# The last down projection third by third of the tokens, with the final norm of five token tiles between its blocks

## What is computed

```python
h2 = _rmsnorm(x, norm2_w) * (1 + scale2) + shift2
f = (jax.nn.silu(h2 @ w_ffn_gate) * (h2 @ w_ffn_up)) @ w_ffn_down
x = x + gate2 * f
...
def _rmsnorm(x, w):
    y = x * lax.rsqrt(jnp.mean(x * x, axis=-1, keepdims=True) + EPS)
    return y * w
```

## Time and profile before

| what | value |
|---|---|
| median of three runs | 2498.18 us (2493.07 to 2500.6) |
| span of the profiled execution | 2492.5 us |
| TensorE busy | 2334.4 us (94%) |
| VectorE busy | 1269.8 us (51%) |
| ScalarE busy | 623.7 us (25%) |
| GpSimd busy | 104.9 us (4%) |
| transfers | 258.75 MB, mean 104 GB/s |

### The profile page before, as it was taken

The page is one execution under the profiler, slowest core; times in us unless marked ns, Lnnn a source line. Parts: engine busy times, 40 slices in busy tenths (PEclk is TensorE's granted clock), DMA queues, the critical chain, the costliest instruction groups (busy, mean ns, idle before and its releaser), DMA issues.

```text
span 2492.5 us, 36698 instructions
## 1 busy us (share of the span) xinstructions
PE 2334.4 (94%) x13811; PEld 2252.1 (90%) x13811; DVE 1269.8 (51%) x2056; ACT 623.7 (25%) x1007; POOL 104.9 (4%) x151
## 2 busy tenths in 40 slices
PE   5699999998899999998999897989999999999995
PEld 5599999998799999988999896879999999999995
DVE  6665544555566767635557545543334434333345
ACT  1423223432333232322121423221111111111111
POOL 0000000000111111101000000010000000000000
PEclk9699999999899999988999998999999999999997
DMA  6265523332555465642223333211111111111104
GB/s 192 71 192 161 169 65 89 89 97 83 176 180 178 157 191 179 199 133 86 87 87 120 108 132 127 85 55 48 42 42 42 42 50 42 42 42 44 48 25 152
DMA packets 319867, 258.75 MB, mean 104 GB/s; under 512 B 13443, under 2 KB 293701, under 8 KB 319807
## 3 DMA queue, kind: packets, MB, share of 16 engines
q1 hardware_dynamic: 263535, 204.11, 27.1%
q10 hardware_dynamic: 52368, 41.57, 5.3%
q0 software_dynamic: 3904, 12.26, 1.4%
HBM read 195.69 MB, written 62.21 MB: 103 GB/s over the span
## 4 chain that ended last, share of the span: by engine, by line
PE 50%; issue 43%; DVE 4%; ACT 1%; DMA 1%; POOL 1%; SPq 0%; ACTq 0%; DVEq 0%; POOLq 0%
PE PS L988 28%; PE PS L1144 11%; PE PS L1126 2%; PE PS L1194 2%; PE PS L1120 1%; PE PS L1123 1%; DVE ada_sum L1382 1%; DVE hf L1400 1%; PE PS L1110 1%; PE PS L1133 1%; PE PS L1029 1%; PE PS L1067 1%; DMA ada_first<-in_w_ada 0%; PE PS L1205 0%; DVE pool_s L1653 0%
## 5 line engine op out<-in xcount | busy, mean ns | idle before, releaser
L988 PE MATMUL PS<-act_a_hi,w_hi 128*128 128x364 f32 (+1 forms) x1344 | 448.4, 334 | 25.2 <-DVE act_a_lo L1613 15.1
L1340 DVE TENSOR_TENSOR w_lo<-w_raw,w_hi 128x1024 fp32r<-128x1024 f32 x156 | 195.5, 1253 | 493.8 <-ACT w_hi L641 492.1
L988 PE MATMUL PS<-act_a_lo,w_hi 128*128 128x364 f32 (+1 forms) x1344 | 445.4, 331 | 0.0
L988 PE MATMUL PS<-act_a_hi,w_lo 128*128 128x364 f32 (+1 forms) x1344 | 445.2, 331 | 0.0
L1286 PE MATMUL PS<-act_b_lo,w_hi 128*128 128x364 f32 (+1 forms) x1056 | 347.7, 329 | 0.0
L1286 PE MATMUL PS<-act_b_hi,w_hi 128*128 128x364 f32 (+1 forms) x1056 | 347.5, 329 | 0.0
L1286 PE MATMUL PS<-act_b_hi,w_lo 128*128 128x364 f32 (+1 forms) x1056 | 347.5, 329 | 0.0
L641 ACT ACTIVATE w_hi<-w_raw 128x1024 fp32r<-128x1024 f32 x156 | 164.7, 1056 | 488.0 <-PE PS L988 213.0
L988 PEld LDWEIGHTS PS<-act_a_hi,w_hi 128*128 128x128 f32 x1344 | 256.2, 191 | 27.8 <-DVE act_a_lo L1613 16.4
L988 PEld LDWEIGHTS PS<-act_a_lo,w_hi 128*128 128x128 f32 x1344 | 256.1, 191 | 0.0
L988 PEld LDWEIGHTS PS<-act_a_hi,w_lo 128*128 128x128 f32 x1344 | 255.9, 190 | 0.0
(11 more groups left out here) (249 smaller groups left out, 3442.2 us busy)
## 6 DMA issues: line engine op xcount, KB each, us to landing
w_raw<-in_w_in SPq DMA_DIRECT2D x64, 512.0 KB, 5.2
acs_in<-acs_c SPq DMA_DIRECT2D x36, 512.0 KB, 5.4
ada<-in_w_ada SPq DMA_DIRECT2D x16, 1024.0 KB, 7.4
gp_s<-gp ACTq DMA_DIRECT2D x24, 544.0 KB, 3.4
w_raw<-in_w_ffn_gate SPq DMA_DIRECT2D x22, 512.0 KB, 3.8
w_raw<-in_w_ffn_up SPq DMA_DIRECT2D x22, 512.0 KB, 3.8
w_raw<-in_w_ffn_down SPq DMA_DIRECT2D x22, 512.0 KB, 3.6
xs_in<-xs_c SPq DMA_DIRECT2D x36, 256.0 KB, 3.0
```

The costliest lines, as they stand in the source:

```text
L988: e = pe.matmul(PS[:, n, 0:w], wt[a], at_[b][:, o:o + w], start=(k == 0 and q == 0), stop=(k == len(steps) - 1 and q == 2))
L1340: dve.tensor_tensor(w_split[v][1][:, :], w_raw[v][:, :], w_split[v][0][:, :].bitcast(F32), ALU.subtract)\
```

## The change

The 24 blocks of the last pair are put in another order: for each third, all eight channel tiles (block i has third i // 8, down unit i // 4 % 2, and PSUM bank i % 3). After 8 blocks the first 364 tokens have their whole sum, which covers token tiles 0 and 1; after 16 blocks 728 tokens, which covers tiles 2, 3 and 4. Their turns stand in TensorE's list behind blocks 9, 11, 17, 19 and 21, and their adds and variances in VectorE's list behind sums 10 to 22. The turns of tiles 5 to 8 stand behind the last block.

SP loads all nine x2 tiles into nine buffers fx of their own as soon as the last up unit is through, then the gain; all nine loads count on one semaphore. The add works in place in fx. For the five early tiles ScalarE multiplies by the power in place, and GpSimd multiplies by the gain in place. For the other four VectorE multiplies by both, as before, but in place. The small per-tile values have a column for each tile (small3). SP stores the tiles in their order.

```diff
+    small3 = keep("small3", [P, 3, NCH])
...
-    (fx0, fx1, fr0, fr1, fjunk, fo0, fo1, final_w) = region(
+    *fx, fjunk, final_w = region(
+        RB, RC, *[(f"fx{t}", [P, KT, P], F32) for t in range(NCH)], ("fjunk", [P, KT, P], F32),
+        ("final_w", [P, KT, P], F32))
...
+    EARLY = 5
+    LAST = [8, 8, 16, 16, 16, 24, 24, 24, 24]
...
-            sp.wait_ge(mm["ffn"], FFN_SUBS)
+            sp.wait_ge(mm["ffn"], FFN_SUBS - 24)
+            for t in range(NCH):
+                L = CH if t < NCH - 1 else DEC
+                sp.dma_start(fx[t][0:L, :, :], x2_s[t][0:L, :].rearrange("t (f c) -> t f c", c=P)).then_inc(f_landed, 16)
             sp.dma_start(final_w[:, :, :], A["final_norm_w"].rearrange("(f c) -> f c", c=P).partition_broadcast(P))\
               .then_inc(fw_in, 16)
...
+            for t in range(NCH):
+                if t < EARLY:
+                    sp.wait_ge(f_pool, t + 1)
+                else:
+                    sp.wait_ge(f_dve, t - EARLY + 1)
...
+            final_power(0)
+            pool.wait_ge(fw_in, 16)
+            for t in range(EARLY):
+                final_power(t + 1)
+                pool.wait_ge(f_scaled, t + 1)
+                pool.tensor_tensor(fx[t][:, :, :], fx[t][:, :, :], final_w[:, :, :], ALU.mult).then_inc(f_pool, 1)
+            for t in range(EARLY + 1, NCH):
+                final_power(t)
...
+            final_squares(0)
+            for t in range(EARLY):
+                final_squares(t + 1)
+                act.wait_ge(f_rms, t + 1)
+                act.activation(fx[t][:, :, :], fx[t][:, :, :], ACT.Copy, scale=small3[:, 2, t:t + 1]).then_inc(f_scaled, 1)
+            for t in range(EARLY + 1, NCH):
+                final_squares(t)
...
-            for v in range(2):
-                down(U_END - 2, FFN_DVE - 24, v)
...
+            def last_down(i):
+                n, v, m = i // 8, i // 4 % 2, i % 4
+                o, w = SUBS[n]
+                unit_ready(U_END - 2 + v)
+                pe.wait_ge(mm_free["ffn"], FFN_DVE - 24 + i + 1)
+                for k in range(2):
+                    for q, (a, b) in enumerate(PASSES):
+                        e = pe.matmul(PS[:, i % 3, 0:w], w_split[v][a][:, k * 512 + m * P:k * 512 + (m + 1) * P],
+                                      f_split[b][:, k, o:o + w], start=(k == 0 and q == 0), stop=(k == 1 and q == 2))
+                e.then_inc(mm["ffn"], 1)
+
+            def final_turn(t):
                 L = CH if t < NCH - 1 else DEC
+                pe.wait_ge(mm_free["ffn"], FFN_DVE - 24 + 3 + LAST[t])
                 if t >= 2:
-                    pe.wait_ge(n3.added, t - 1)
+                    pe.wait_ge(f_added, t - 1)
...
+            turn_after = {9: 0, 11: 1, 17: 2, 19: 3, 21: 4}
+            for i in range(24):
+                last_down(i)
+                if i in turn_after:
+                    final_turn(turn_after[i])
+            for t in range(EARLY, NCH):
+                final_turn(t)
...
+            def final_add(t):
+                L = CH if t < NCH - 1 else DEC
+                if t == 0:
+                    dve.wait_ge(f_landed, 16 * NCH)
+                dve.wait_ge(f_turned, t + 1)
...
+            add_after = {10: 0, 12: 1, 18: 2, 20: 3, 22: 4}
+            var_after = {12: 0, 14: 1, 20: 2, 22: 3}
+            for i in range(24):
+                last_sum(i)
+                if i in var_after:
+                    final_var(var_after[i])
+                if i in add_after:
+                    final_add(add_after[i])
             dve.wait_ge(fw_in, 16)
...
+            for t in range(EARLY, NCH):
+                final_add(t)
+                final_var(t - 1)
+                if t > EARLY:
+                    final_scale(t - 1)
+            final_var(NCH - 1)
+            final_scale(NCH - 1)
```

More of the change, by code:

```diff
@@ L470, in _ @@
                 load_unit(U_END - 2 + v, v, wd[:, 2 * FG - 2:2 * FG, v * 512:(v + 1) * 512])
-            sp.wait_ge(mm["ffn"], FFN_SUBS)
+            sp.wait_ge(mm["ffn"], FFN_SUBS - 24)
+            for t in range(NCH):
+                L = CH if t < NCH - 1 else DEC
+                sp.dma_start(fx[t][0:L, :, :], x2_s[t][0:L, :].rearrange("t (f c) -> t f c", c=P)).then_inc(f_landed, 16)
             sp.dma_start(final_w[:, :, :], A["final_norm_w"].rearrange("(f c) -> f c", c=P).partition_broadcast(P))\
               .then_inc(fw_in, 16)
[L476 to L485, removed]
-            for v in range(2):
[L488 to L499, removed]
+            for t in range(NCH):
[4 more added lines that the diff above has]
+                L = CH if t < NCH - 1 else DEC
+                dst = yo_p[t * CH:(t + 1) * CH, :] if t < NCH - 1 else yo_s
+                sp.dma_start(dst.rearrange("t (f c) -> t f c", c=P), fx[t][0:L, :, :]).then_inc(out_sem, 16)
+            sp.wait_ge(out_sem, 16 * NCH)
         @block.gpsimd
@@ L619, in norm2_tiles @@
                     powers(n2, t, v, L)
-            def norm3_tiles(tiles, L):
-                for t, v, i in tiles:
-                    powers(n3, t, v, L)
             pairs(norm2_tiles)
@@ L965, in _, with final_squares @@
             hi(U_END - 1, 1, "ffn", FFN_SUBS - 24)
[L968 to L976, removed]
+            def final_squares(t):
+                L = CH if t < NCH - 1 else DEC
+                act.wait_ge(f_added, t + 1)
+                act.wait_ge(f_squared, t)
+                act.activation(fjunk[0:L], fx[t][0:L], ACT.Square, accum_out=small3[0:L, 0, t:t + 1]).then_inc(f_squared, 1)
+            final_squares(0)
[5 more added lines that the diff above has]
+                final_squares(t)
         @block.tensor
@@ L1847, in _ @@
             dve.wait_ge(mm_free["ffn"], FFN_DVE - 24)
[L1848 to L1861, removed]
-                                         final_w[0:L, :, :], ALU.mult, ALU.mult).then_inc(n3.scaled, 1)
@@ L1878, in _, with last_sum @@
-            norm3_scale(8, 0, 64, DEC)
+            def last_sum(i):
+                n, f = i // 8, i % 8
+                o, w = SUBS[n]
+                dve.wait_ge(mm["ffn"], FFN_SUBS - 24 + i + 1)
+                parts = [(o, w, 0)] if o + w <= SEQ else [(o, SEQ - o, 0), (SEQ, DEC, 1)]
+                for at_, n_, q in parts:
+                    dst = acc[:, f, at_:at_ + n_]
+                    e = dve.scalar_tensor_tensor(dst, PS[:, i % 3, at_ - o:at_ - o + n_], mods[:, GATE2 + f, q:q + 1], dst,
+                                                 ALU.mult, ALU.add)
+                e.then_inc(mm_free["ffn"], 1)
```

53 lines of the change are left out of this document (25 added, 28 removed).

## The result

| | before | after |
|---|---|---|
| median of four runs | 2496.26 us (2493.07 to 2500.6) | 2477.51 us (2476.38 to 2481.99) |
| ratio, 95% interval | 1 | 0.9926 [0.9912, 0.9941] |
| span of the profiled execution | 2492.5 us | 2480.3 us |
| time of that execution | 2494.33 us | 2481.99 us |

The change takes 0.74% off. Nothing that the change touches lies ahead of that mark. Before it is 2492.5 - 2421.66 = 70.8 us, after it is 2480.3 - 2424.52 = 55.8 us: 15.1 us less, where the prediction's sum said 14.7.

A forecast was written before the change was run, and what follows sets the result against it. It took the end after the last sum, a chain of final-norm steps waiting for x2 and engine handovers, as the bound. The end shrinks 14.7 us: 2498.2 - 14.7 = 2483.5 us, range 2475 to 2491.

The forecast's parts named there:

- the prediction's sum: Over the kernel's end: last scaling at 2474.3 instead of 2489.1 us, 14.8 less, rounded with the span to 14.7.
- the prediction's new end: Steps after the last down-projection sum at 2456.2 us: turns, adds, powers, products, scalings and last store, to span 2477.8 us.
- Block stage, 5.0 us later: Last 24 down-projection blocks: with five early turns, adds and variances among them, the last sum ends at 2456.2 us.
- The cover of the other adds: In the last blocks, early adds hide under TensorE's matmuls; the rival without cover: 5.7 us more, time 2489.2, chance 0.05.
- x2 there 1.6 us ahead: Nine loads before the first add: 2.8 us start and landing plus 12.8 at 348 GB/s, landed at 2437.3 us.
- x2 late: Rival on the loads before the first add: at 219 GB/s, span 2483.1 and time 2488.8 us; chance 0.06.
- Product 2.2 us: GpSimd's multiplication of an early tile by the gain, 128x1024: taken as twice a one-input pass, 2.2 us.
- The lock: At the end, GpSimd's product 4 delays VectorE's scaling 5 through shared SBUF ports; without it span 2475.5, not 2477.8 us.
- The low bound's span of 2474.4: Whole kernel with a GpSimd product of 1.1 us: time 2480.1 us; with the spread of runs, low bound 2475.
- The end: After the last sum at 2456.2 us: last scaling ends at 2474.3, last store adds 3.4, span 2477.8 us.
- turns at full clock: TensorE's transposes behind the last block run at full clock after 1.9 us rest; at 0.50 the end comes 0.9 later.
- carry the difference over: Whole kernel: the 14.7 us saved in the profiled span is taken off the median, 2498.2 to 2483.5 us.

The follow-up runs named there:

- late loads: Changed kernel with the loads of x2 and the gain issued when four of the 24 last blocks are through: 2489.33 us in one run, stretch 64.0 us.
- both edits: Changed kernel with the gain in PSUM for VectorE's four scalings, and those scalings one add later in its list: 2475.12 us, stretch 51.2 us.
- scalings later: Changed kernel with VectorE's scalings at the end one add later in its list: 2475.88 us, stretch 52.9 us.

## Why the prediction was right, and where it was off

The forecast was 2483.5 us, faster; it came to 2477.5, inside the range. Times of the prediction's new end are shifted here by 2.86 us, by which the mark stands later in the profile after.

*Block stage, 5.0 us later:* 5.3. Without early tiles the last sum ends 29.6 us behind the mark, with two turns 31.3, with five 34.7. Two turns are thus 1.7, about twice 0.79; five are 3.95 and 1.2 more, most of which is add 4 (with it behind sum 23 only 0.35 is left). The cover of the other adds held: no gap on TensorE among the blocks.

*x2 there 1.6 us ahead:* 1.3, by the late loads. But the two terms behind it were both off. The changed kernel's table by stretches has the rate, and its transfers from 2420 to 2450 us, in slices of 0.75 us, have the course:

```profile
2430.00:2435.00 5.00, 5.00 (x26) 5.00 (x25) 2.38 (x4) 0.00 (x0) 0.00 (x0) 0.79 1.02 413
...
GB/s 0 0 0 0 0 0 0 131 273 393 410 410 437 415 410 415 415 431 399 404 410 410 158 202 295 186 60 11 0 0 0 0 0 0 0 0 0 0 0 0
```

At 413 GB/s instead of 348 the 4.46 MB are some 10.8 us instead of 12.8, so 5.1 of the 15.9 lie at the two ends and not 2.8. Some 2.2 us pass from the first issue until 393 GB/s are reached, and from 2436.5, when some 4.3 of the 5.0 MB (with the gain row, which is queued behind the loads) have moved, the rate is only 158 to 295. Why the far end is slow is not shown; the gain row may have a part in it. SP's issuing of the nine loads, 4.42 us, does not set the time: 410 GB/s are reached while it still issues. The two errors nearly cancelled, which was luck: four blocks' delay alone turns the case into the rival "x2 late". In that rival the prediction let the banks hide 0.7 of a hold of 6 us; in the late loads a hold of 7.5 us cost 8.2, so nothing was hidden.

*Product 2.2 us:* 2.36 to 2.42. The estimate from the Trainium skill (GPSIMD Engine Reference, section 3.1), 2.25 us, was a little nearer, and the trace lies 0.14 above it too. Power 5 behind product 3 and the hold of scaling 5 by product 4 came as told: scaling 5 was due to end at 2468.5 and ended at 2468.64. The prediction let it start behind the product and take 1.3; the record has it start at once and take 3.35, ending 1.08 after product 4. The lock was priced at 2.3 us (2477.8 against 2475.5); with the gain in PSUM the stretch was 2.0 shorter. The low bound's span of 2474.4 leaves this hold out: with it the same steps come to 2475.6 for a product of 1.1 us, and nothing hangs on it.

*The end:* turns at full clock, which the prediction took without a row that has such a rest, and which the granted clock of 1.00 up to 2460 us, with 1.65 us of rest in it, bears out; 17.65 us from the last sum to the last scaling instead of 18.1, 3.4 to the last store. The sum over the stretch was 0.4 us off.

*The median:* here is the step that missed, "carry the difference over". The median fell by 18.75 us, the stretch by 15.06. The median of before came to 2496.26 with a fourth run, which is 1.9 of the 6.0 us between forecast and result; 0.4 is the stretch; the other 3.7 are, as far as the profiled runs tell, in no place that the change touches; the other runs left no trace. The mark, up to which all these kernels do the same work, stood between 2416.5 (both edits) and 2425.6 us (scalings later) in the eleven profiles other than the one of before, whose mark is at 2421.66. The four runs of after have granted clocks of 0.963, 0.966, 0.972 and 0.974 in order of falling time. So a median of four runs can lie a few microseconds off for reasons ahead of the mark, and the profiled run of after was the longest of its four. Why the clock granted earlier in the program varies was not tried.

## What to carry to other kernels

When work is moved under matmuls onto an idle in-order engine, the place of its small steps in that engine's list decides as much as their length: a power listed ahead of a long product waited for something that came only after the matmuls, and made two early tiles worth 1 us instead of 4.7. Look for a VectorE op with two SBUF inputs beside GpSimd work, and put one operand in PSUM (2.07 us here). And when the change is a fraction of a percent, compare a stretch between a mark that nothing touches and the end; it told versions apart that the medians could not.

## What the runs showed of the hardware that was not expected

- Loads of 4 KB rows ran at 413 GB/s beside full matmuls; 348 in the earlier row was no ceiling.
- The lock between VectorE and GpSimd holds even a 128x1 power: 1.55 us instead of 0.55 beside a scaling.
- A VectorE op held by a product ends 1.08 us after it, less than its own 1.28.
- With the late loads, TensorE's granted clock was 0.55 from 2450 to 2455 after 6.1 us without work; in the changed kernel it was 1.00 from 2450 to 2460 in spite of 1.65 us without work.
